# Round border filled earlier, and leaf inverses of 16x16 joined on TensorE, in a two-layer decoder trunk

## The reference, cut to what matters

```python
CHUNK = 64
g_cum = jnp.cumsum(log_alpha, axis=-1)
decay = jnp.exp(jnp.where(causal, g_cum[..., :, None] - g_cum[..., None, :], -jnp.inf))
a = jnp.where(strict, jnp.einsum('bhnld,bhnsd->bhnls', k_beta, k) * decay, 0.0)
rhs = jnp.concatenate([v * beta[..., None], k_beta * jnp.exp(g_cum)[..., None]], axis=-1)
sol = lax.linalg.triangular_solve(a, rhs, left_side=True, lower=True, unit_diagonal=True)
# then a scan over the chunks with q_g, w, u, attn, k_tail
```

## Time and profile before

| | |
|---|---|
| median of 3 runs | 2863.43 us (2860.95 to 2864.47) |
| profiled execution | 2861.21 us, span 2859.4 us |
| TensorE matmuls | 2788.6 us busy, 98% |
| VectorE | 1569.4 us, 55% |
| ScalarE | 1368.2 us, 48% |
| granted TensorE clock | 0.996 of full speed |

### The profile page before, as it was taken

How to read it: one execution, slowest core, us unless ns; L and a number is a source line. 1 busy time by engine, 2 the same in 40 slices (tenths; PEclk the granted TensorE clock), 3 DMA queues, 4 the chain that set the end, 5 groups by cost and what they waited for, 6 DMA issues and landing times.

```text
span 2859.4 us, 37257 instructions
## 1 busy us (share of the span) xinstructions
PE 2788.6 (98%) x13652; PEld 2298.6 (80%) x13652; DVE 1569.4 (55%) x1942; ACT 1368.2 (48%) x1874; POOL 74.2 (3%) x55
## 2 busy tenths in 40 slices
PE   8999999999999999998999999999999999999998
PEld 6788788888888888886878787887888888888886
DVE  4554565545445445458586768665554454454444
ACT  5354455444444444455665656554454444444443
POOL 0000000000000000000000010000000000000000
PEclk9999999999999999999999999999999999999999
DMA  7464466666666666654454545555666666666664
GB/s 235 147 199 151 136 191 185 192 190 187 190 187 191 187 189 191 181 167 135 123 157 126 153 128 156 162 169 185 189 185 194 188 190 189 187 191 189 206 191 141
DMA packets 261266, 502.63 MB, mean 176 GB/s; under 512 B 20112, under 2 KB 20368, under 8 KB 260624
## 3 DMA queue, kind: packets, MB, share of 16 engines
q1 hardware_dynamic: 259504, 494.60, 58.0%
q0 software_dynamic: 816, 3.15, 0.3%
q10 hardware_dynamic: 816, 3.15, 0.3%
HBM read 495.59 MB, written 5.24 MB: 175 GB/s over the span
## 4 chain that ended last, share of the span: by engine, by line
PE 86%; DVE 7%; ACT 4%; issue 1%; DVEq 1%; ACTq 0%; DMA 0%; SPq 0%
PE acc L533 27%; PE acc L527 26%; PE acc L528 26%; DVE wlo L1386 2%; PE aux L759 2%; PE aux L580 2%; DVE arena L1785 1%; ACT whi L957 1%; DVE arena L1782 1%; DVE arena L1747 1%; PE aux L765 1%; DVE const L1747 1%; ACT arena L1302 0%; DVEq L1784 0%; DVEq L1751 0%
## 5 line engine op out<-in xcount | busy, mean ns | idle before, releaser
L1386 DVE TENSOR_TENSOR wlo<-wraw,whi 128x1024 fp32r<-128x1024 f32 x928 | 1151.4, 1247 | 1111.4 <-ACT whi L957 1102.9
L957 ACT ACTIVATE whi<-wraw 128x1024 fp32r<-128x1024 f32 x928 | 974.1, 1060 | 1096.0 <-PE acc L533 1043.9
L527 PE MATMUL acc<-whi,hT_hi 128*128 128x512 f32 x2624 | 1039.8, 396 | 7.5 <-ACT whi L957 7.1
L528 PE MATMUL acc<-whi,hT_lo 128*128 128x512 f32 x2624 | 1024.3, 390 | 0.0
L533 PE MATMUL acc<-wlo,hT_hi 128*128 128x512 f32 x2624 | 708.0, 392 | 27.9 <-DVE wlo L1386 27.2
L533 PEld LDWEIGHTS acc<-wlo,hT_hi 128*128 128x128 f32 x2624 | 489.7, 188 | 146.3 <-DVE wlo L1386 45.8
L527 PEld LDWEIGHTS acc<-whi,hT_hi 128*128 128x128 f32 x2624 | 493.9, 188 | 109.8 <-issue 7.9
L528 PEld LDWEIGHTS acc<-whi,hT_lo 128*128 128x128 f32 x2624 | 494.1, 188 | 100.8 <-issue 1.0
L527 PE MATMUL acc<-whi,arena 128*128 128x512 f32 x1088 | 428.4, 394 | 3.2 <-ACT whi L957 3.2
L528 PE MATMUL acc<-whi,arena 128*128 128x512 f32 x1088 | 425.8, 391 | 0.0
L533 PE MATMUL acc<-wlo,arena 128*128 128x512 f32 x1088 | 293.4, 391 | 0.0
(11 more groups left out here) (239 smaller groups left out, 1172.9 us busy)
## 6 DMA issues: line engine op xcount, KB each, us to landing
wraw<-in_l_w_in SPq DMA_DIRECT2D x304, 512.0 KB, 3.8
wraw<-in_l_w_gate SPq DMA_DIRECT2D x176, 512.0 KB, 3.7
wraw<-in_l_w_up SPq DMA_DIRECT2D x176, 512.0 KB, 3.7
wraw<-in_l_w_down SPq DMA_DIRECT2D x176, 512.0 KB, 4.1
wraw<-in_l_w_out SPq DMA_DIRECT2D x96, 512.0 KB, 4.6
o_rounds<-arena POOLq DMA_DIRECT2D x3, 1024.0 KB, 4.8
arena<-o_rounds ACTq DMA_DIRECT2D x3, 1024.0 KB, 6.2
x<-in_x SPq DMA_DIRECT2D x4, 512.0 KB, 6.0
```

The lines of the kernel that those rows point to most:

```text
L527: nc.tensor.matmul(pair[m], hi[:, k, tok], wh, start=first, stop=False)
L528: nc.tensor.matmul(pair[m], lo[:, k, tok], wh, start=False, stop=False)
L957: nc.scalar.activation(whi[:, s, :], wraw[:, s, :], ACT.Copy).then_inc(hi_done, 1)
L1386: V.tensor_tensor(wlo[:, s, :], wraw[:, s, :], whi[:, s, :].bitcast(F32), ALU.subtract).then_inc(lo_done, 1)
```

## The change

The decays of a round are computed in slots -6 and -5, that is in slots 31 and 32 of the round before (round 0: -2 and 0). K's transposes and tap go from slot 0 to slot -1, V0's from 7 to 1 (into `aux[1]`), V0's `conv` on VectorE from 9 to 2, its silu from 11 to 5; K's `silu` from 3 to 2. The turned decays go from slots 4 and 7 to 7 and 9. On VectorE, the two 16x16 blocks on the diagonal of each 32x32 one are inverted at once (15 steps in slots 10 to 17); GpSimd cuts out the corner between them (`corner`), and TensorE joins them with 64 and 128 matmuls of 32x32 (`join_q`, `join_t`) in slots 18 and 19. The constant table changes with it.

```diff
+DECAYS_AT = lambda r, c: (-2, 0)[c] if r == 0 else (-6, -5)[c]
...
+        conv_psum = (aux[0], aux[1], aux[0], aux[0])
...
+                pool.wait_ge(diag_set, r + 1)
+                nc.gpsimd.tensor_tensor(corner[:], diag[:], C["corner"].unsqueeze(1).to_broadcast([P, M * HV, LEAF]), ALU.mult
+                                        ).then_inc(corner_set, 1)
...
+                def join_q(to):
+
+                    for n in range(M * HV):
+                        for b in range(4):
+                            mm = nc.tensor.matmul(to[quarter(b), n * LEAF:(n + 1) * LEAF], corner[quarter(b), n, :], leaf_TT[quarter(b), n, :],
+                                                  start=True, stop=True)
+                    mm.then_inc(join_psum, 1)
...
+                def join_t(to, to_t):
+
+                    for n in range(M * HV):
+                        for b in range(4):
+                            nc.tensor.matmul(to[quarter(b), n * LEAF:(n + 1) * LEAF], Q16[quarter(b), n, :], leaf_T[quarter(b), n, :],
+                                             start=True, stop=True)
+                        for b in range(4):
+                            mm = nc.tensor.matmul(to_t[quarter(b), n * LEAF:(n + 1) * LEAF], leaf_T[quarter(b), n, :], Q16[quarter(b), n, :],
...
-                if s == 0:
+                if s == DECAYS_AT(r, 0):
                     if r:
-                        pe.wait_ge(end_dve, END_DVE(r - 1, "o1"))
+                        pe.wait_ge(lev_sub, LEVEL_SUB(r - 1, "TT64_1"))
                     else:
                         pe.wait_ge(gate_step, GATE_AT["sums_exp"])
                     decays(0, aux[1])
+                if s == DECAYS_AT(r, 1):
+                    pe.wait_ge(d_exp, D_AT(r, 0))
+                    decays(1, aux[1])
+                if s == -1:
                     if r:
                         pe.wait_ge(end_act, END_ACT(r - 1, "vn1"))
                     conv_transposes(K, aux[0])
-                if s == 2:
-                    pe.wait_ge(d_exp, D_AT(r, 0))
-                    decays(1, aux[1])
+                if s == 1:
+                    if r:
+                        pe.wait_ge(end_dve, END_DVE(r - 1, "o1"))
+                    pe.wait_ge(d_exp, D_AT(r, 1))
+                    conv_transposes(V0, aux[1])
                 if s == 4:
-                    pe.wait_ge(d_exp, D_AT(r, 1))
-                    decays_turned(0, aux[1])
                     pe.wait_ge(conv_sum, TOK_AT(r, K))
                     token_major(K, aux[0])
                 if s == 5:
-                    pe.wait_ge(et_copy, D_AT(r, 0))
+                    pe.wait_ge(conv_sum, TOK_AT(r, V0))
                     products(4, aux[1])
                 if s == 7:
                     pe.wait_ge(gram_mask, GRAM_AT(r, "kk"))
+                    decays_turned(0, aux[1])
+                if s == 8:
+                    pe.wait_ge(tok_copy, TOK_AT(r, K))
+                    token_major(V0, aux[0])
+                if s == 9:
+                    pe.wait_ge(et_copy, D_AT(r, 0))
                     decays_turned(1, aux[1])
-                    pe.wait_ge(tok_copy, TOK_AT(r, K))
-                    conv_transposes(V0, aux[0])
-                if s == 13:
-                    pe.wait_ge(conv_sum, TOK_AT(r, V0))
-                    token_major(V0, aux[0])
                 if s == 15:
                     pe.wait_ge(tok_copy, TOK_AT(r, V0))
                     conv_transposes(Q, aux[0])
                 halves = [aux[1][:, c * NB:(c + 1) * NB] for c in range(M)]
+                if s == 18:
+                    pe.wait_ge(et_copy, D_AT(r, 1))
+                    pe.wait_ge(corner_set, r + 1)
+                    pe.wait_ge(solved, r + 1)
+                    join_q(halves[0])
+                if s == 19:
+                    pe.wait_ge(join_copy, r + 1)
+                    join_t(halves[1], halves[0])
...
+                    if r < ROUNDS - 1:
+                        pe.wait_ge(d_exp, D_AT(r + 1, 1))
...
+                for c in range(M):
+                    if s == DECAYS_AT(r, c):
+                        exps(c)
+                if s == -1:
                     tap(K)
+                if s == 1:
+                    tap(V0)
                 if s == 2:
-                    exps(1)
-                if s == 3:
                     silu(K)
                 if s == 4:
-                    turned(0)
                     act.wait_ge(tok_tr, TOK_AT(r, K))
                     nc.scalar.activation(flat(k_tok[:]), aux[0][:, :], ACT.Copy)
                     act.drain()
                     squares(K, 0)
                 if s == 5:
                     nc.scalar.activation(small(2, 8, 8), small(2, 0, 8), ACT.Sqrt, bias=epsc[:, 0:1], scale=1.0).then_inc(root_set, 1)
+                    silu(V0)
                 if s == 7:
+                    turned(0)
+                if s == 9:
                     turned(1)
-                    tap(V0)
-                if s == 9:
                     act.wait_ge(a_set, D_AT(r, 1))
                     if r:
                         act.wait_ge(o_stored, 16 * r)
@@ -1246,12 +1298,13 @@
                     if r == ROUNDS - 1:
                         act.wait_ge(conv_tr, TOK_AT(r, V0))
                         load_o(0)
-                if s == 11:
-                    silu(V0)
-                if s == 13:
+                if s == 10:
                     value_rows(V0)
                 if s == 15:
                     tap(Q)
+                if s == 18:
+                    act.wait_ge(join_psum, JOIN_PSUM(r, "q16"))
+                    nc.scalar.activation(Q16[:].rearrange("p k n -> p (k n)"), aux[1][:, 0:NB], ACT.Copy).then_inc(join_copy, 1)
...
-                                diag[:].rearrange("p k j -> p j k").unsqueeze(2).to_broadcast([P, LEAF, 2, LEAF // 2]))
-                    V.tensor_copy(leaf_t[:].rearrange("p i c -> p (i c)"), C["leaf_eye"])
+                    V.transpose(lead[:].rearrange("p j i -> p (j i)"), diag[:].rearrange("p k (e j) -> p j e k", e=2))
+                    V.tensor_copy(solve_t[:].rearrange("p i c -> p (i c)"), C["solve_eye"])
+                    dve.drain()
+                    V.tensor_scalar(solve_a[:], lead[:, :, 0:SOLVE], half(0), None, ALU.mult)
+                    dve.drain()
+                    V.scalar_tensor_tensor(solve_a[:], lead[:, :, SOLVE:], half(1), solve_a[:], op0=ALU.mult, op1=ALU.add)
                     dve.drain()
 
                 def leaf(first, last):
 
                     for j in range(first, last):
-                        rows, cols = LEAF - 1 - j, j // 2 + 1
+                        rows, cols = SOLVE - 1 - j, j + 1
                         p = leaf_p[:, 0:rows * cols].rearrange("p (i c) -> p i c", c=cols)
-                        below = leaf_t[:, j + 1:, 0:cols]
-                        V.tensor_tensor(p, lead[:, j, j + 1:].unsqueeze(2).to_broadcast([P, rows, cols]),
-                                        leaf_t[:, j:j + 1, 0:cols].to_broadcast([P, rows, cols]), ALU.mult)
+                        below = solve_t[:, j + 1:, 0:cols]
+                        V.tensor_tensor(p, solve_a[:, j, j + 1:].unsqueeze(2).to_broadcast([P, rows, cols]),
+                                        solve_t[:, j:j + 1, 0:cols].to_broadcast([P, rows, cols]), ALU.mult)
                         dve.drain()
                         V.tensor_tensor(below, below, p, ALU.subtract)
                         dve.drain()
 
                 def leaf_end():
-                    V.transpose(leaf_T[:].rearrange("p k (c e) -> p c e k", e=2), leaf_t[:].rearrange("p i c -> p c i")
-                                ).then_inc(leaf_set, 1)
-                    dve.drain()
-                    V.transpose(leaf_TT[:].rearrange("p k i -> p (k i)"), leaf_T[:].rearrange("p k j -> p (k j)")).then_inc(leaf_set, 1)
+
+                    for e in range(2):
+                        V.tensor_scalar(spread[:, e * SOLVE:(e + 1) * SOLVE, :], solve_t[:], half(e), None, ALU.mult)
+                    dve.drain()
+                    V.transpose(leaf_T[:].rearrange("p k (e c) -> p c e k", e=2), spread[:].rearrange("p i c -> p c i"))
+                    dve.drain()
+                    dve.wait_ge(corner_set, r + 1)
+                    V.transpose(leaf_TT[:].rearrange("p k i -> p (k i)"), leaf_T[:].rearrange("p k j -> p (k j)")).then_inc(solved, 1)
+                    dve.drain()
+
+                def leaf_join():
+
+                    dve.wait_ge(join_psum, JOIN_PSUM(r, "T16"))
+                    for to, n in ((leaf_T, 1), (leaf_TT, 0)):
+                        V.tensor_tensor(to[:], to[:], aux[1][:, n * NB:(n + 1) * NB].rearrange("p (k n) -> p k n", n=LEAF), ALU.subtract
+                                        ).then_inc(leaf_set, 1)
 
                 quarter_of = lambda x: x.rearrange("p (h n) -> p h n", n=HALF)
 
@@ -1801,8 +1871,10 @@
```

(29 more changed lines are left out.)

24 lines of the change are left out of this document (13 added, 11 removed).

## The result

The kernel after takes 2895.2 us (median of 4, 2890.8 to 2897.0) against 2864.0 for the kernel before in the same session: a ratio of 1.0111, 95% interval 1.0098 to 1.0123. It is slower by 31 us; 2863.8 was predicted, and the range ended at 2873. The profiled execution took 2890.79 us, span 2889.0, granted clock 0.992.

A forecast was written before the change was run, and what follows sets the result against it. TensorE was taken as the bound, idle 32.75 us of 594.40 in the rounds. -41.3 + 18.1 + 0.4 + 11.5 + 10.0 = -1.3 us, with a clock fall (+1.7) +0.4: median 2863.8 us, 0.8 range 2851 to 2873.

The forecast's parts named there:

- Outside the rounds nothing is changed.: Phases outside the four rounds: claimed to be untouched by the change, so no term in the sum.
- Joins, 18.1 us: TensorE, `join_q` and `join_t`: 1.76 + 2.76 = 4.5 us added a round, four quarters abreast; 18.1 in all.
- Clock, one fall as before: Granted clock in the rounds: one fall behind a wait counted again, +1.7 us, as in round 1 before.
- the rival: Clock falls at every join: five more falls (four joins, one border) at 1.7 us, 2872.3; chance 0.17.
- Waits won: TensorE's old waits in the rounds: 43.3 us less 2.0 that stays, so 41.3 us to be won.
- waits for the join: TensorE ahead of `join_q`, waiting for `solved`: 2.3 us a round, 4.7 in round 3; 11.5 in all.
- border: Round border: new TensorE waits for `wlo` in unit 5 and the Gram mask before slot 7; 10.0 us in all.
- extra burst: TensorE: moving decays, transposes and turned copies leaves one more burst standing alone, 0.1 us a round, 0.4 in all.
- 35 waits: TensorE's waits in the rounds before the change, whose hidden time was put at 5.6 us.
- rule of 0.16 us each: TensorE's pauses in the trace: each shows 0.16 us short, a record of 0.39 against a spacing of 0.23.
- VectorE in time: Slot 18: wait for the join gone in rounds 0 to 2, halved in round 3, no clock fall; 2852.9; chance 0.28.
- Quarters not abreast: Joins on TensorE: two quarters abreast gives +12.1 us, 2875.9; serial 36 more than forecast; chance 0.10.

The follow-up runs named there:

- split_20: Kernel after with `join_t` cut in two: the `leaf_TT` matmuls and Q's convolution in slot 20, `leaf_join` in slot 21; 2880.1 us, ratio 1.0063.
- before_arena_64: Kernel before with only the arena moved 64 bytes further on, to byte 133248; 2855.0 us, ratio 0.9972.
- before_arena_128: Kernel before with only the arena moved 128 bytes further on, to byte 133312; 2876.4 us, one execution.
- half_t_later: Kernel after with half of `join_t`, joins in slots 19 and 20, Q's convolution in 20, `leaf_join` in 21, arena 64 bytes further; 2863.4 us, ratio 0.9998.
- after_split_t: Kernel after with `join_t` cut in two: the `leaf_TT` matmuls and `leaf_join` in slot 21, Q's convolution in slot 22; 2900.3 us.
- half_t_later_placed: half_t_later with only the arena's start changed, to byte 133248 instead of 132352; 2846.1 us, ratio 0.9944.

## Why the prediction was wrong

Against the profiled execution of before, the forecast was +0.4 us and the trace shows +29.6. By the steps of the prediction:

- **"Outside the rounds nothing is changed."** This step failed first and cost most: +14.5 us. The constant table changes with the change, the arena lies behind it, and a unit whose stationary operand is in the arena costs 0.053 us more; 272 units. Shown in both kernels and in both directions.
- **Joins, 18.1 us.** The cost of a step abreast was right: `join_q` with four quarters abreast shows 128 records in 1.28 us, and unit 18 less its wait costs 1.4 to 1.6 us over its usual 2.7, against 1.76 forecast; in split_20 each half of `join_t` costs 1.4 to 1.5. Mis-sized was `join_t`: its instructions are not there in time. 9.9 us of `issue`, for which the sum had nothing. I had priced a burst of 512 instructions from bursts of 128 and 192, which showed no hole.
- **Clock, one fall as before.** The forecast's net was nothing; the half clock cost 8.2 us in the rounds instead of 1.0 (one fall costs 0.8 to 2.6 us here; 1.7 was forecast). Part of it hangs on the holes (3.5 us are left with half of `join_t`). Behind three of the four waits for `solved` the clock fell, nearly as the rival had it (2872.3); behind the same four waits in split_20 it fell once, so how often it does is not settled. The Trainium skill ("TensorE: Matmul & The Clock Gate", Part 1) has the clock drop to half after idling; the trace agrees in that all six stretches at half clock stand behind an idle stretch of TensorE, of 2.0 to 4.3 us.
- **Waits won, waits for the join, border.** Right. The join waited 2.3, 2.0, 2.0 and 4.3 us (2.3, 2.3, 2.3 and 4.7 forecast), the mask 3.2, 0.4, 1.5 and 0.4 (2.9, 0.5, 1.8, 0.5), unit 5 1.8, 1.2 and 1.2 (2.1, 1.1, 1.1). All slots of l1 but 18 to 20 gained 23.7 us; the forecast's terms for them give 21.0 (39.6 of waits, less the 8.2 us that slots 18 to 20 lost before, less 10.4 for the border and the extra burst). One reading was short: the prediction counts 35 waits before, while the trace has four more, 1.4 us ahead of the turned decays (L746); by its own rule of 0.16 us each that is 0.6 us more to win.
- **Two rivals.** VectorE in time: fell, the wait for `solved` is there. Quarters not abreast: fell for four quarters in one bank, which run at 0.010 us a record. The rule of the Trainium skill ("TensorEngine Tiling (Array Packing)", Restrictions and Gotchas) that different row tiles cannot access one PSUM bank at once is not borne out by these joins, in which each quarter writes 32 partitions of its own; no run has row tiles that write the same partitions.

The sum then: 0.4 of the forecast, 14.5 for the place, 9.9 for the holes, 7.4 for the half clock in slots 18 to 20, less 1.2 for a cheaper `join_q`, 0.9 for the shorter join wait and 2.7 for the other slots, is 27.4. The other 2.2 of the 29.6 us lie in slots 18 to 20 and are not attributed.

The two halves together: the moves are worth nothing (1.0003), the joins cost 11 us (1.0041), the address 14.5. That is about 26 of 31 us. The other 5 come only where both halves are in one kernel: with the arena in its old place both take 2879.4 us and the joins alone 2874.3, with a wait for `solved` of 10.5 us against 8.1 and holes of 11.8 against 10.0; what makes them so is not shown.

With the joins a slot later, half of `join_t` and the arena moved, the same idea is 0.65% faster than before. Not all of that is the idea's: the kernel before gains 0.28% by the address alone (before_arena_64). Against that kernel the best one is ahead by 0.4%, taken over two sessions, and 4.9 us of holes are still in it.

Open is when TensorE's next packet of instructions is asked for, and so why one round has a hole of 0.3 us and another of 3.9; the holes moved between rounds from kernel to kernel. Open too is what in the memory makes the distance between the operands count.

## What to carry to other kernels

A change that resizes a table moves what lies behind it: print the offsets of the matmul operands before and after, and compare the pace of unchanged phases by counts in windows of one length, since the busy share stays at 100%. Before pricing a burst of small matmuls by its rows, count its instructions (four for each float32 matmul here), and spread hundreds of them over several slots of wide work, or let another engine make half of the result. Look at the trace afterwards: with the halved burst the holes fell to 0.8 us in one kernel and were 4.1 to 5.2 us in the three with the joins a slot later. A version that gains by an address is to be compared with the old kernel at that address. When a total contradicts a theory, read the slots: one run here was slower in sum though the holes that it should close were closed.

## What the runs showed of the hardware

- The pace of a stream of 128x512 matmuls depends on the distance of its stationary operand from its moving operand, counted within 512 (perhaps 256) bytes of a partition: 2.720 us for 12 at 0 (before_arena_64), 2.747 at -64 (before), 2.800 at +64 (after, before_arena_128), 2.78 to 2.80 at 128 (half_t_later). But for the last the usual unit is the same to 0.001 us in every kernel; over 272 units it makes 21 us between the two ends in the kernel before (2855.0 and 2876.4), 0.75%.
- TensorE's instructions come in packets of 16 KB, 256 each. In the joins of the kernel after the packets start 3.4 us and more apart (3.3 in after_split_t). Its burst of 512, which at the pace of `join_q` (256 in 1.28 us) would want them in 2.6 us, stood still for 0.3 to 3.9 us, and went on 1.0 to 1.5 us after the packet had landed. Bursts of 256 stood too, up to 2.7 us (half_t_later_placed).
- 32x32 float32 matmuls in four quarters of the array, all into one PSUM bank, each into its own 32 partitions, run abreast: 128 records in 1.28 us, against 64 in 1.20 for two quarters.
